# Seven-product block groups in the gate and up products of a two-layer trunk kernel

## What is computed

```
gate, up = _split(rms_norm(x, norm_ffn[i]) @ w_gate_up[i], (D_FF, D_FF))   # D_MODEL 2048, D_FF 5632
x = x + (jax.nn.silu(gate) * up) @ w_down[i]
```

## Time and profile before

| | |
|---|---|
| median of 3 runs | 2190.85 us |
| the profiled execution, its own time | 2190.48 us |
| its span, first to last instruction | 2188.8 us |
| TensorE matmuls | busy 2175.4 us, 99% of the span, 10172 instructions |
| VectorE | busy 1293.3 us, 59% |
| ScalarE | busy 1029.5 us, 47% |
| granted TensorE clock | 1.000 all through |
| read from memory | 411.25 MB, 189 GB/s over the span |

### The profile page before, as it was taken

The page is one execution under the profiler, slowest core; times in us unless marked ns, Lnnn a source line. Parts: engine busy times, 40 slices in busy tenths (PEclk is TensorE's granted clock), DMA queues, the critical chain, the costliest instruction groups (busy, mean ns, idle before and its releaser), DMA issues.

```text
span 2188.8 us, 29206 instructions
## 1 busy us (share of the span) xinstructions
PE 2175.4 (99%) x10172; PEld 1811.1 (83%) x10172; DVE 1293.3 (59%) x1555; ACT 1029.5 (47%) x1310; POOL 58.7 (3%) x99
## 2 busy tenths in 40 slices
PE   8999999999999999999999999999999999999999
PEld 7888888888888888888888888888888888888887
DVE  6767766555555555555566767675555555554443
ACT  7755654444444444444444445454444444443332
POOL 2101100000000000000100000000000000000000
PEclk9999999999999999999999999999999999999999
DMA  8765476766676666666555656577666766666664
GB/s 311 239 194 154 135 214 208 212 202 202 204 211 204 204 198 198 209 204 202 178 173 163 198 166 190 163 221 221 202 202 205 210 204 204 200 213 203 202 203 133
DMA packets 244562, 435.48 MB, mean 199 GB/s; under 512 B 23040, under 2 KB 43648, under 8 KB 244480
## 3 DMA queue, kind: packets, MB, share of 16 engines
q1 hardware_dynamic: 243392, 432.31, 64.8%
q10 hardware_dynamic: 1088, 2.10, 0.2%
HBM read 411.25 MB, written 2.10 MB: 189 GB/s over the span
## 4 chain that ended last, share of the span: by engine, by line
PE 99%; ACT 0%; DVE 0%; DMA 0%; issue 0%; DVEq 0%; SPq 0%; ACTq 0%
PE unit_bank L1629 95%; PE mix_bank L1652 1%; PE mix_bank L1782 1%; PE mix_bank L1717 0%; PE mix_bank L1679 0%; PE mix_bank L1726 0%; PE mix_bank L1768 0%; DVE w_lo L1005 0%; DMA source_T<-in_mem_T 0%; PE mix_bank L1690 0%; PE mix_bank L1701 0%; PE mix_bank L1813 0%; PE mix_bank L1811 0%; PE mix_bank L1804 0%; PE mix_bank L1794 0%; ACT p_a L675 0%
## 5 line engine op out<-in xcount | busy, mean ns | idle before, releaser
L1005 DVE TENSOR_TENSOR w_lo<-raw,w_hi 128x1024 fp32r<-128x1024 f32 x767 | 932.2, 1223 | 757.9 <-ACT w_hi L582 738.1
L582 ACT ACTIVATE w_hi<-raw 128x1024 fp32r<-128x1024 f32 x767 | 808.9, 1060 | 904.8 <-PE unit_bank L1629 875.4
L1629 PE MATMUL unit_bank<-w_hi,hT_hi 128*128 128x512 f32 (+1 forms) x1984 | 615.0, 391 | 0.0
L1629 PE MATMUL unit_bank<-w_hi,hT_lo 128*128 128x512 f32 (+1 forms) x1984 | 610.2, 389 | 0.0
L1629 PE MATMUL unit_bank<-w_lo,hT_hi 128*128 128x512 f32 (+1 forms) x1984 | 609.8, 389 | 0.0
L1629 PEld LDWEIGHTS unit_bank<-w_hi,hT_lo 128*128 128x128 f32 x1984 | 372.3, 188 | 76.5
L1629 PEld LDWEIGHTS unit_bank<-w_lo,hT_hi 128*128 128x128 f32 x1984 | 372.3, 188 | 76.5
L1629 PEld LDWEIGHTS unit_bank<-w_hi,hT_hi 128*128 128x128 f32 x1984 | 368.8, 188 | 72.8 <-DVE w_lo L1005 0.2
L1629 PE MATMUL unit_bank<-w_hi,gT_hi 128*128 128x512 f32 x704 | 217.0, 389 | 0.0
L1629 PE MATMUL unit_bank<-w_lo,gT_hi 128*128 128x512 f32 x704 | 216.9, 389 | 0.0
L1629 PE MATMUL unit_bank<-w_hi,gT_lo 128*128 128x512 f32 x704 | 216.8, 389 | 0.0
(11 more groups left out here) (232 smaller groups left out, 1028.3 us busy)
## 6 DMA issues: line engine op xcount, KB each, us to landing
raw<-in_w_gate_up SPq DMA_DIRECT2D x352, 512.0 KB, 4.3
raw<-in_w_down SPq DMA_DIRECT2D x176, 512.0 KB, 4.5
raw<-in_w_in_b SPq DMA_DIRECT2D x104, 512.0 KB, 4.0
raw<-in_w_o SPq DMA_DIRECT2D x64, 512.0 KB, 4.4
raw<-in_w_in_a SPq DMA_DIRECT2D x40, 512.0 KB, 4.1
moved<-turned SPq DMA_DIRECT2D x528, 32.0 KB, 3.1
raw<-in_w_mem_kv SPq DMA_DIRECT2D x31, 512.0 KB, 5.6
tanh_ff<-act_ff SPq DMA_DIRECT2D x112, 32.0 KB, 3.3
```

The costliest lines, as they stand in the source:

```text
L582: act.activation(w_hi[:, s, :, :], raw[:, s, :, :], ACT.Copy).then_inc(sems["hi_ready"], 1)
L1005: dve.tensor_tensor(w_lo[:, s, :, :], raw[:, s, :, :], w_hi[:, s, :, :].bitcast(F32), ALU.subtract).then_inc(sems["lo_ready"], 1)
L1629: ins = pe.matmul(unit_bank[2 * pair + tile][:, 0:cols], stationary[part][:, kt + j, tile * P:(tile + 1) * P], b[:, s, j, 0:cols], start=o ...
```

## The change

In each of the ten looped chunks two of the eight pairs of pieces (`SEVEN = (2, 5)`) are multiplied in a Strassen-like way. A pair of pieces holds the blocks of one pair of features k, k+1: gate and up, so the product is a 2 x 2 block of X (two token tiles by two feature blocks) times a 2 x 2 block of W. Done plainly that is eight block products of three matmuls; the new form needs seven, of sums of blocks: sums and differences of X made once a layer (`seven_forms`), sums of W made for every group (`split_seven`), and four of the seven products shared between outputs, so that they accumulate in banks of their own. These are the parts of the change:

1. Gate and up pieces now alternate (SyncE's queue, `chunk_turns`), and the four banks of a chunk (`own`) hold gate and up of both tiles. The other four banks hold the shared products (`shared`). `unit_bank` and `mix_bank` swap these parts with every chunk, so the hardware loop now does two chunks a turn. The first chunk of a layer goes to `mix_bank` with all its products plain.
2. A group's two pieces are split together. ScalarE rounds three raw blocks in one instruction, then four sums in three; VectorE makes the low parts of three raw blocks, four sums and four low parts, in seven instructions.
3. At a chunk's end VectorE forms the outputs: four instructions on the shared banks in step 13 (`shared_products`), four on the own banks behind the chunk (`own_products`). ScalarE copies one shared bank in step 12. The results lie in SBUF, so `gate_tanh` and `gate_silu` move to step 1 of the next chunk, `times_up` with the transposes to step 5, the 16 small transfers behind pieces 11, 12 and 13 (6, 6 and 4 of them), and `moved_block` to step 14.

The diff, cut to its core. The transfers of a chunk:

```diff
+SEVEN = (2, 5)
...
-                with t.loop(1, CHUNKS_FF, {"lo_ready": KT, "turned_ready": 1}) as j:
-                    unit(wg, j * COLS)
-                    unit(wg, j * COLS + D_FF, between=moves({n: (4 * n, 4 * n + 4) for n in range(4)}))
+                chunk_turns = moves({11: (0, 6), 12: (6, 12), 13: (12, 16)})
+                with t.loop(0, CHUNKS_FF // 2, {"lo_ready": 2 * CHUNK_PIECES, "turned_ready": 2}) as j:
+                    for half in range(2):
+                        for n in range(CHUNK_PIECES):
+                            piece(wg, n // 2 * 2, j * (2 * COLS) + (1 + half) * COLS + n % 2 * D_FF)
+                            chunk_turns(n)
```

ScalarE's split of a group:

```diff
+            def split_seven():
+
+                s = slot[0] % RING
+                slot[0] += 2
+                for n in (s, s + 1):
+                    act.wait_ge(sems[f"arrived{n}"], t.next(f"arrived{n}", 16))
+                t.move("split", 2)
+                act.wait_ge(sems["piece_used"], t.value("split", RING))
+                act.activation(four_blocks(w_hi, s)[:, 1:4, :], four_blocks(raw, s)[:, 1:4, :],
+                               ACT.Copy).then_inc(sems["hi_ready"], 2)
+                act.wait_ge(sems["sum_ready"], t.next("sum_ready"))
+                act.activation(sums_hi[:, :, :], sums[:, :, :], ACT.Copy).then_inc(sems["sum_hi_ready"], 1)
+                act.wait_ge(sems["sum_ready"], t.next("sum_ready"))
+                act.activation(w_hi[:, s, 0, :], w_sum[:, s, 0, :], ACT.Copy).then_inc(sems["sum_hi_ready"], 1)
+                act.wait_ge(sems["lo_ready"], t.value("split"))
+                act.activation(sum_all_hi[:, :], sum_all[:, :], ACT.Copy).then_inc(sems["sum_hi_ready"], 1)
+
+            def chunk_pieces():
+
+                for i in range(CHUNK_PIECES):
+                    yield i
+                    ahead = (i + LEAD) % CHUNK_PIECES
+                    if ahead // 2 not in SEVEN:
+                        split()
+                    elif ahead % 2 == 0:
+                        split_seven()
+                    t.move("at")
```

ScalarE's chunk:

```diff
-                def chunk(j):
-                    for i in pieces(8):
-                        pass
-                    gate_tanh()
-                    for i in pieces(8):
+                def chunk(j, shared):
+                    for i in chunk_pieces():
                         if i == 1:
-                            moved_block(gT, (j - 1) * 4)
-                    act.wait_ge(sems["piece_used"], unit_done(other))
+                            gate_tanh()
+                        if i == 12:
+                            act.wait_ge(sems["piece_used"], t.value("at"))
+                            act.activation(up_ff[:, 0, :], shared[0][:, :], ACT.Copy).then_inc(sems["first_copied"], 1)
+                        if i == 14:
+                            moved_block(gT, j * 4)
```

VectorE's split of a group, its chunk, and what it does at the chunk's end:

```diff
+            def split_seven():
+
+                s = slot[0] % RING
+                slot[0] += 2
+                dve.wait_ge(sems["hi_ready"], t.next("hi_ready", 2))
+                t.move("split", 2)
+                dve.wait_ge(sems["piece_used"], t.value("split", RING))
+                blocks, low, high = (four_blocks(ring, s) for ring in (raw, w_lo, w_hi))
+                dve.tensor_tensor(low[:, 1:4, :], blocks[:, 1:4, :], high[:, 1:4, :].bitcast(F32),
+                                  ALU.subtract).then_inc(sems["raw_lo_ready"], 1)
+                dve.tensor_tensor(sums[:, :, :], blocks[:, 1:3, :], blocks[:, 0:1, :].broadcast_to([P, 2, COLS]),
+                                  ALU.add).then_inc(sems["sum_ready"], 1)
+                dve.wait_ge(sems["sum_ready"], t.next("sum_ready"))
+                dve.tensor_tensor(w_sum[:, s, 0, :], sums[:, 1, :], blocks[:, 1, :], ALU.add).then_inc(sems["sum_ready"], 1)
+                dve.wait_ge(sems["sum_ready"], t.next("sum_ready"))
+                dve.tensor_tensor(sum_all[:, :], w_sum[:, s, 0, :], blocks[:, 3, :], ALU.add).then_inc(sems["lo_ready"], 2)
+                dve.wait_ge(sems["sum_hi_ready"], t.next("sum_hi_ready"))
+                dve.tensor_tensor(sums_lo[:, :, :], sums[:, :, :], sums_hi[:, :, :].bitcast(F32),
+                                  ALU.subtract).then_inc(sems["sum_lo_ready"], 1)
+                dve.wait_ge(sems["sum_hi_ready"], t.next("sum_hi_ready"))
+                dve.tensor_tensor(w_lo[:, s, 0, :], w_sum[:, s, 0, :], w_hi[:, s, 0, :].bitcast(F32),
+                                  ALU.subtract).then_inc(sems["sum_lo_ready"], 1)
+                dve.wait_ge(sems["sum_hi_ready"], t.next("sum_hi_ready"))
+                dve.tensor_tensor(sum_all_lo[:, :], sum_all[:, :], sum_all_hi[:, :].bitcast(F32),
+                                  ALU.subtract).then_inc(sems["sum_lo_ready"], 1)
...
+                def shared_products(shared):
...
+                    dve.tensor_tensor(act_ff[:, 1, :], shared[3][:, :], up_ff[:, 0, :], ALU.subtract).then_inc(sems["dve_chain"], 1)
+                    dve.wait_ge(sems["dve_chain"], t.next("dve_chain"))
+                    dve.tensor_tensor(act_ff[:, 0, :], shared[1][:, :], act_ff[:, 1, :], ALU.add)
+                    dve.tensor_tensor(up_ff[:, 1, :], shared[2][:, :], act_ff[:, 1, :], ALU.add).then_inc(sems["dve_chain"], 1)
+                    dve.wait_ge(sems["dve_chain"], t.next("dve_chain"))
+                    dve.tensor_tensor(act_ff[:, 1, :], shared[1][:, :], up_ff[:, 1, :], ALU.add).then_inc(sems["own_free"], 1)
...
+                def chunk(j, own, shared):
+
+                    for i in chunk_pieces():
                         if i == 1:
-                            moved_block(gT, (j - 1) * 4, "gT_ready")
-                    times_up()
+                            gate_silu()
+                        if i == 5:
+                            times_up()
+                        if i == 13:
+                            shared_products(shared)
+                        if i == 14:
+                            moved_block(gT, j * 4, "gT_ready")
+                    own_products(own)
```

TensorE's group:

```diff
+            def product(bank, x_parts, w_hi_block, w_lo_block, start, stop):
+                for m, (part, w) in enumerate(((0, w_hi_block), (1, w_hi_block), (0, w_lo_block))):
+                    ins = pe.matmul(bank[:, :], x_parts[part], w, start=start and m == 0, stop=stop and m == 2)
+                return ins
+
+            def seven_products(n, own, shared):
+
+                s = slot[0] % RING
+                slot[0] += 2
+                t.move("lo_ready", 2)
+                kt, first, last = 2 * SEVEN[n], n == 0, n == len(SEVEN) - 1
+                x11, x12, x22 = ([h[:, k, tile * P:(tile + 1) * P] for h in hT] for k, tile in ((kt, 0), (kt + 1, 0), (kt + 1, 1)))
+                x21_less_x11 = [h[:, kt, P:2 * P] for h in hT]
+                form = [[f[:, n, m, :] for f in forms] for m in range(3)]
+                pe.wait_ge(sems["raw_lo_ready"], t.next("raw_lo_ready"))
+                product(own[1], x12, w_hi[:, s + 1, 1, :], w_lo[:, s + 1, 1, :], False, False)
+                product(own[0], form[2], w_hi[:, s, 1, :], w_lo[:, s, 1, :], False, False)
+                if first:
+                    pe.wait_ge(sems["shared_free"], t.next("shared_free"))
+                product(shared[0], x11, w_hi[:, s + 1, 0, :], w_lo[:, s + 1, 0, :], first, last)
+                pe.wait_ge(sems["sum_lo_ready"], t.next("sum_lo_ready"))
+                product(shared[1], form[0], sums_hi[:, 1, :], sums_lo[:, 1, :], first, last)
+                product(shared[2], x21_less_x11, sums_hi[:, 0, :], sums_lo[:, 0, :], first, last)
+                pe.wait_ge(sems["sum_lo_ready"], t.next("sum_lo_ready"))
+                product(shared[3], form[1], w_hi[:, s, 0, :], w_lo[:, s, 0, :], first, last)
+                pe.wait_ge(sems["sum_lo_ready"], t.next("sum_lo_ready"))
+                product(own[3], x22, sum_all_hi[:, :], sum_all_lo[:, :], False, False).then_inc(sems["piece_used"], 2)
```

185 lines of the change are left out of this document (146 added, 39 removed).

## The result

The changed kernel takes **2178.24 us** (median of 4 runs, 2177.48 to 2179.54), the kernel before 2190.9 us in the same session. The ratio is 0.9944, 95% interval 0.9929 to 0.9958: 12.7 us or 0.6% faster. The forecast was 2177.

What follows compares the result with a forecast made beforehand. TensorE, busy 99% of the span, was taken as the bound: matmul count times spacing. 2190.5 - 27.2 (120 matmuls fewer) + 13.5 (waits in 18 chunks) = 2176.8, said as 2177 us, range 2164 to 2194.

Steps and rivals of the forecast that it cites:

- Matmuls that go: Gate and up groups: 3 of 24 matmuls fewer in each, 120 in all at 0.2267 us, saving 27.2 us.
- The rival of wider spacing: Three matmuls in a row into one bank are spaced wider in groups: 2163 plus up to 91 us; chance 0.02.
- The group's own chain: From the first matmul two pieces ahead of a group, 7.21 us until its fourth product may start; 0 lost.
- the margin of 0.04: Fourth product's weight load is due at 7.25 us, its parts at 7.21, if VectorE is free in time.
- VectorE's backlog: At a chunk's end VectorE runs 13.2 us without gap, so the next group's low parts start at 7.9, not 7.16.
- The landing of piece 15: Piece 15, issued directly behind piece 14, lands 35.3 to 36.2 us into the chunk; 35.8 was taken.
- A wait of 0.75 us at the fourth product of a chunk's first group: TensorE waits there, 0.25 to 1.15 us by the landing, in 9 chunks x 2 layers: 13.5 us.
- VectorE alone as what ends last ahead of the group: Ahead of a first group, VectorE's queue without a gap sets the low parts' start, 7.9 where 7.16 was due.
- No wait at all: Piece 15 lands in 3.5 + 1.0 us and TensorE does not wait: 2163.3, up to 2167 us; chance 0.17.
- Late transfers for the second group: Pieces 8 to 11 land too late for the second group's split: 41 us lost, 2204 us; level 0.10, slower 0.11.
- Free edits: Forms of X, first chunk's copies, last chunk's own products, last tanh, silu and turns cost nothing.
- signs of being wrong: Second-group waits, ScalarE waiting for transfers ahead of a group, group spacing over 0.23, or waits summing under 5 us.

Runs made afterwards that it cites:

- the eighth experiment: Changed kernel with four small transfers behind each of pieces 11 to 14, sums' high products first, down product's gT wait at its piece 18: 2163.59 us, ratio 0.9876.
- the seventh kernel, experiment 7: Changed kernel with the 16 small transfers on GpSimd's queue and the high products of the sums first: 2163.51 us, ratio 0.9875 against the kernel before.
- experiments 2: Changed kernel with the 16 small transfers of every looped chunk issued by GpSimd instead of SyncE: 2167.3 us, ratio 0.9895 against the kernel before.
- 5: Changed kernel with four small transfers behind each of pieces 11, 12, 13 and 14 on SyncE's queue: 2166.43 us, ratio 0.9888 against the kernel before.
- 6: Changed kernel with four small transfers behind each of pieces 12, 13, 14 and 15 on SyncE's queue: 2167.26 us, ratio 0.989 against the kernel before.
- experiment 4: Changed kernel with the four matmuls on the sums' high parts ahead of those on low parts: 2175.58 us, ratio 0.9929 against the kernel before.
- experiment 3: Changed kernel with VectorE's silu moved behind the first group's seven instructions: 2198.2 us, ratio 1.0034 against the kernel before.

## Why the prediction was right, and where not

*Matmuls that go.* Right: 120 fewer, and three matmuls in a row into one bank keep their spacing (641.21, 641.44; a chunk of 42.16 us in the eighth experiment). The rival of wider spacing is out. Gate and up of a layer last 478.72 us before and 465.12 in the seventh kernel: 13.60 us for 60 matmuls, 226.7 ns each. By the rule of the Trainium skill (TensorE: Matmul & The Clock Gate, section "Back-to-back issue gap") 25.9 us would go in all, as an estimate. The section calls its 216 ns that of an isolated matmul and gives some 131 ns for 512 columns in a stream of weight loads and matmuls; the trace agrees with neither.

*The group's own chain.* Mis-sized by 0.2 us. From the first matmul of the piece two ahead of the group to the end of the sums' low parts I had 7.21; from 377.86 to 384.06 + 1.22 it is 7.42. ScalarE starts 0.26 behind that matmul, not 0.20; VectorE's low parts begin 0.12 behind ScalarE's end, not 0.03; the fourth sum comes 0.79 behind the third, not 0.72. So instead of the margin of 0.04 the weight load of the fourth product is 0.2 late. The matmul itself still comes in its place (385.34), and the next one 0.33 behind it instead of 0.227. Together this is 0.03 to 0.15 a group in most chunks, 3.5 us in all: what experiments 2, 5 and 6 keep, and what the order of the products removes in 7 and 8. I took 0, with 0 to 0.1 as the range.

*VectorE's backlog.* The mechanism and its cause held: forecast from the group to piece 14's issue 23.0 us, measured 23.1; from piece 15's low part to the next group 13.2, measured 13.2. The landing of piece 15 was mis-sized: it came 4.3 after its issue, 4.9 after that of piece 14, where I took 5.6; ScalarE's copy of a shared bank ahead of the rounding, which I left out, gave 0.3 of it back. So the next group begins 42.65 behind the last, not 42.9.

*"A wait of 0.75 us at the fourth product of a chunk's first group", in 18 chunks.* This step failed in its form and was saved by its sum. The product was late in just these 18 chunks, but by 0.04 to 0.57 us. The lost time was 13.6 us against 13.5, but only 8.2 of it at the first group. The numbers I had were those of a cycle, and I used the excess of it as the lateness at one wait, less that wait's margin. A margin doesn't come off a cycle (experiment 4). The excess shows at whichever wait is tightest at that time: the first group, pieces 14 and 15, and the begin of the down product. The last two I hadn't looked at. Piece 14 lands at 663.2 and its low part is ready at 665.6, for a piece whose first weight load is due at 665.7. The smaller excess (0.5 for 0.78) and the waits that I took for nothing (the groups' own, 3.5 us, and 1.6 before the down product, where the backlog reaches gT) made up for each other. 13.6 against 13.5 is partly luck.

*VectorE alone as what ends last ahead of the group.* Wrong by omission: piece 5's transfer and ScalarE end at the same time. A remedy by the forecast's picture (experiment 3) made the fourth product less late by 1.3 us in all and cost 20, most of it at piece 6.

*Rivals.* No wait at all did not come, but is what the eighth experiment makes. Late transfers for the second group: 1.4 us lost there instead of 41; in the two chunks where it lost 0.2 us ScalarE had waited for a transfer, in the others under 0.1 was lost, and alone it loses 0.03 a chunk, so this rival is out. *Free edits:* the forms of X cost nothing in gate and up (the first chunk lasts 43.52 in both layers). Not forecast were 0.8 us at the very first matmul, which comes at 8.0 to 9.0 in the profiles of these kernels, so that it need not belong to the change, and 0.5 us elsewhere. Some 0.16 of these are the second matmul of each down product, 0.305 us behind the first; for the rest I have no cause.

*Signs.* Two of the signs of being wrong came with a time that was right: waits in the second groups, 1.4 us, and ScalarE waiting for transfers ahead of a group, 16 times and 22.7 us in all. VectorE is busy 37.1 us in the chunk shown and 1555 in all, not 39.7 and 1600: the forecast added the instructions from start to end, and so added they make 39.5 in that chunk, but they overlap.

## What to carry to other kernels

When one engine is full and the others feed it in a loop, add up the loop from one point round to the same point in the next turn, with every queue it passes. If that is longer than the full engine's work, each turn costs the difference, wherever the wait shows, and more margin at the wait only moves it; take time out of the cycle, and only then tighten the waits. Before work is moved out of the way of one wait, look at what is due next behind its new place: here that cost 20 us. Small transfers in front of a large one on the same queue are part of such a cycle; here spreading them over one more piece was worth 12 us. And before a second saving of the same kind is added, see whether the first has used up the slack.

## What the runs showed of the hardware

In the changed kernel the fourth product of a group came 0.04 to 0.57 us late 20 times, and the matmul behind it came 0.334 to 0.341 us later instead of 0.227, so that such a wait costs 0.11 us more than its length. It isn't so at every wait: of ten late first matmuls of plain pieces six were followed like this, while four that were 0.06 to 0.12 us late were followed after 0.225 to 0.240 us, and the two down products after 0.305.

GpSimd issued a small transfer every 0.49 us (SyncE needs 0.62). But after every 21 of them, counted through the whole execution, the next came only 2.4 to 4.8 us behind, 15 times; in experiment 7 it was again 15 times, behind the same transfers, at 2.2 to 4.5 us. One such place in GpSimd's timeline of experiment 2, and its transfers' row in the page (KB each, median us from issue to landing):

```profile
645.49 4.39 POOL L601 DMA_DIRECT2D moved<-turned  x9 [30.88 <-DVE turned L1182]
654.00 1.00 POOL L601 DMA_DIRECT2D moved<-turned  x2 [4.12 <-issue]
```

```profile
moved<-turned POOLq DMA_DIRECT2D x320, 32.0 KB, 3.5
```

The pauses come by the count of the transfers, not with a certain instruction of VectorE. They did no harm, since gT was in time.

The Trainium skill (SBUF — State Buffer, section "SBUF: two separate sides") says that GpSimd can't write descriptors while VectorE runs an operation that takes the port they share, such as an fp32 copy in SBUF. The same section counts operations with two inputs in SBUF among these only against a GpSimd operation that reads SBUF. VectorE's subtractions of the low parts are fp32 operations with two inputs in SBUF, and no run here has a stall that follows them: the spacing stayed 0.49 us while they ran. What takes the port the trace doesn't tell.
